# Squares of the decay in a bidirectional gated linear recurrence: from GpSimd with two places to ScalarE with four

## What is computed

```python
def rglru_gates(u, wa, ba, wx, bx, lam):
    r = sigmoid(blockdiag(u, wa) + ba)
    i_g = sigmoid(blockdiag(u, wx) + bx)
    log_a = -LRU_C * r * softplus(-lam)
    a = exp(log_a)
    b = sqrt(-expm1(2.0 * log_a)) * (i_g * u)
    return a, b
# h_t = a_t * h_(t-1) + b_t, over the context first, then over the latent tokens,
# once forwards and once backwards; the two results are added and gated
```

## Time and profile before

| | |
|---|---|
| median of 3 runs | 2322.23 us (2318.98 to 2324.4) |
| profiled execution, its own time | 2321.31 us |
| its span, first to last instruction | 2319.5 us |
| mean granted TensorE clock | 0.92 |
| busy share of the span: PE, DVE, ACT, POOL | 83%, 49%, 34%, 14% |
| the scan stage in the span | about 1388 to 1575 us |

### The profile page before, as it was taken

One profiled execution on the slowest core, in us unless ns is written; L12 is line 12 of the kernel. 1 busy time (PEld: TensorE's weight loads), 2 busy tenths in 40 slices (PEclk: granted clock), 3 DMA queues, 4 the chain that ended last, 5 costly groups with the idle time before them and its releaser, 6 DMA issues. The chain is left out here.

```text
span 2319.5 us, 33553 instructions
## 1 busy us (share of the span) xinstructions
PE 1913.9 (83%) x9971; PEld 1296.5 (56%) x9972; DVE 1148.0 (49%) x2243; ACT 792.0 (34%) x1283; POOL 317.4 (14%) x333
## 2 busy tenths in 40 slices
PE   2899997889999999999975887637778787788883
PEld 0778844467777777777742881103445555555551
DVE  2325622577777777777748565893131121111124
ACT  1214511155555556555521456870101111111110
POOL 0220010021211111121110102221001111111110
PEclk9999997989999999999987997768879999999997
DMA  6850054069999899999956416304439999999994
GB/s 240 282 202 2 1 224 180 32 230 333 340 332 339 324 339 348 346 334 343 336 179 249 136 47 202 110 19 131 183 145 415 407 402 404 404 404 392 409 381 173
DMA packets 139045, 597.07 MB, mean 257 GB/s; under 512 B 32632, under 2 KB 51128, under 8 KB 79728
## 3 DMA queue, kind: packets, MB, share of 16 engines
q1 hardware_dynamic: 103264, 509.97, 58.5%
q0 software_dynamic: 35584, 84.31, 9.8%
q10 hardware_dynamic: 144, 2.10, 0.2%
HBM read 596.17 MB, written 56.20 MB: 281 GB/s over the span
## 5 line engine op out<-in xcount | busy, mean ns | idle before, releaser
L1459 DVE TENSOR_TENSOR m_w_lo<-m_wgu,m_w_hi 128x1024 fp32r<-128x1024 f32 x264 | 314.0, 1221 | 157.3 <-ACT m_w_hi L1383 146.3
L1383 ACT ACTIVATE m_w_hi<-m_wgu 128x1024 fp32r<-128x1024 f32 x264 | 269.7, 1053 | 192.9 <-DMA m_wgu<-in_moe_w_up 135.2
L1630 PE MATMUL ps<-m_wgu,m_xT 128*64 128x256 f32 x2112 | 263.0, 405 | 77.4 <-DMA m_wgu<-in_moe_w_up 57.0
L1630 PEld LDWEIGHTS ps<-m_wgu,m_xT 128*64 128x64 f32 x2112 | 187.3, 146 | 164.0 <-issue 117.2
L1325 PE MATMUL ps<-m_wd,m_hidT 128*128 128x512 f32 x528 | 237.6, 593 | 0.3 <-ACT m_hidT L1407 0.3
L1340 PE MATMUL ps<-m_w_hi,m_x_hi 128*128 128x512 f32 x528 | 212.7, 403 | 7.1 <-DVE m_x_lo L1451 7.0
L1340 PE MATMUL ps<-m_w_lo,m_x_hi 128*128 128x512 f32 x528 | 208.1, 394 | 0.0
L1340 PE MATMUL ps<-m_w_hi,m_x_lo 128*128 128x512 f32 x528 | 207.2, 392 | 0.0
L1725 DVE SCALAR_TENSOR_TENSOR m_hid<-m_act_g,m_meta,ps 128x256 f32<-128x256 f32 x33 | 15.8, 480 | 337.7 <-ACT m_act_g L1679 337.7
L1325 PEld LDWEIGHTS ps<-m_wd,m_hidT 128*128 128x128 f32 x528 | 95.3, 190 | 95.1 <-issue 95.1
L1266 POOL DMA_INDIRECT y_rows<-h,m_sidx x66 | 67.5, 1023 | 552.8 <-DVE h L1467 552.8
(11 more groups left out here) (317 smaller groups left out, 3420.5 us busy)
## 6 DMA issues: line engine op xcount, KB each, us to landing
m_wgu<-in_moe_w_gate SPq DMA_DIRECT2D x132, 1024.0 KB
m_wgu<-in_moe_w_up SPq DMA_DIRECT2D x132, 1024.0 KB
m_wd<-in_moe_w_down SPq DMA_DIRECT2D x132, 1024.0 KB, 9.7
c_rows<-y_rows SPq DMA_DIRECT2D x12, 2048.0 KB, 16.1
mods<-in_ada_w POOLq DMA_DIRECT2D x11, 1024.0 KB, 7.3
mods<-in_ada_w SPq DMA_DIRECT2D x11, 1024.0 KB, 4.8
mods<-in_lru_w_in SPq DMA_DIRECT2D x7, 1280.0 KB, 6.9
ada_w<-in_ada_w SPq DMA_DIRECT2D x8, 1024.0 KB, 17.8
```

Source lines behind the costliest of these rows:

```text
L1383: act.activation(w_hi[:, :, k, :], wgu[:, q, :, k, :], ACT.Copy).then_inc(hi_s, 1)
L1459: dve.tensor_tensor(w_lo[:, :, k, :], wgu[:, q, :, k, :], w_hi[:, :, k, :].bitcast(F32), ALU.subtract).then_inc(lo_s, 1)
L1630: last = pe.matmul(g.ps[half[s], GU, a * FE:(a + 1) * FE], xT[:, k, half[s]], wgu[:, s, a, k, :], start=(k == 0), stop=(k == KD - 1))
```

## The change

ScalarE makes the square of each block's decay right behind its exponential and tangent, with a wait for the complement of block j-4. GpSimd's loop goes away. The squares get a tensor of their own with four places instead of two places in a row of `g.h`.

```diff
-        sq = g.h[0:RW, 2, :].rearrange("p (b c) -> p b c", c=TOK)
+        sq = sb("sq", [RW, 4, TOK])
...
                         act.activation(r[:, q, :], r[:, q, :], ACT.Tanh, bias=pos4[:, c:c + 1], scale=pos4[:, c:c + 1]).then_inc(exps, 1)
+                        if j >= 4:
+                            act.wait_ge(omts, j - 3)
+                        act.activation(sq[:, j % 4, :], a[:, q, :], ACT.Square).then_inc(sqs, 1)
...
-                for j in range(len(blocks)):
-                    n = j % SLOTS
-                    pool.wait_ge(exps, 2 * j + 1)
-                    if j >= 2:
-                        pool.wait_ge(omts, j - 1)
-                    pool.tensor_tensor(sq[:, j % 2, :], a[:, n, :], a[:, n, :], ALU.mult).then_inc(sqs, 1)
...
-                        dve.scalar_tensor_tensor(r[:, j % SLOTS, :], sq[:, j % 2, :], 1.0, r[:, j % SLOTS, :], ALU.add, ALU.mult).then_inc(omts, 1)
+                        dve.scalar_tensor_tensor(r[:, j % SLOTS, :], sq[:, j % 4, :], 1.0, r[:, j % SLOTS, :], ALU.add, ALU.mult).then_inc(omts, 1)
```

## The result

The changed kernel is slower by a ratio of 1.0025 (95% interval 1.0016 to 1.0034), which is +5.8 us on 2320.06 (+3.7 to +7.9). The medians of 20 runs each are 2325.39 and 2320.06 us. The forecast was +5.9 us and 2328.1 us; the three runs shown before the forecast had a median 2.2 us above that of all twenty, and the medians themselves differ by 5.3 us, 0.5 less than the ratio says.

What follows compares the result with a forecast made beforehand. ScalarE was taken to set the pace until VectorE takes over in groups 6 to 8. Squares +12.6, clock +1.6, first `finish` -1.45, groups 6, 7, 8 -2.57, -3.38, -0.9: +5.9 us, 2328.1 us, range 2323 to 2334.

Steps and rivals of the forecast that it cites:

- Price of a square: On ScalarE: 0.525 us a square, 2.10 for four, ends 0.45 and 0.81; 24 squares in the lead, +12.6 us.
- The new wait: On ScalarE before a square, for the complement of block j-4: claimed never to hold.
- Hidden squares: Group 3's squares (2.10 us) fall into block 18's gate-read wait; group 7's are hidden by VectorE's scans.
- Groups 6, 7, 8: Last groups of the scan stage: net shifts of -0.47, -3.38 and -0.9 us as VectorE's work gets shorter.
- First finish: Group 3: scans to `finish` need 8.44 us instead of 9.89, -1.45; block 18's gate-read wait shrinks to 1.2.
- Clock in group 0: TensorE's pause before block 7 grows to 3.35 us, putting that block at the low clock level: +1.6 us.
- rival 1: The clock in group 0 stays high: +4.3 us, 2326.5, a result inside 0.2%; chance 0.22.
- Rivals 2, 3 and 4: Squares dear as tangents, 2332.8 to 2334.9, chance 0.12; VectorE leads from group 4, 2316.4, 0.06; table loads, about 2405, 0.02.
- rival 5: Part of the shift is lost later, where TensorE's clock changes at another instant: 2322 to 2326 us; chance 0.08.

Runs made afterwards that it cites:

- E5: The changed kernel with two places for the squares on ScalarE instead of four; 1.0069 of the kernel before, +16.0 us.
- E1: The kernel before, GpSimd's squares kept, with ScalarE making a second set that nobody reads; ratio 1.004 to the kernel before, +9.3 us.
- E10: The kernel before, unchanged, traced a second time; its scan stage took 147.53 us, group 3 20.32 us.
- E2: The kernel before with the squares left out, the complement reading the decay itself; 0.9959 of the kernel before, -9.5 us.

## Why the prediction was right, step by step

- **Price of a square:** 0.525 forecast, 0.52 measured, 24 of them in the lead: groups 1, 2, 4 and 5 grew by 2.08 each. The new wait never holds (0.0 us); with two places it does (E5).
- **Hidden squares:** those of groups 3, 7 and 8, and in group 6 ScalarE's wait of 2.57 us, which hides its four. E1 confirms it: there they cost nothing in group 3 and in groups 6 to 8.
- **Groups 6, 7, 8:** -0.51, -3.36, -0.80 against -0.47, -3.38, -0.9.
- **First finish:** scans to `finish` took 8.37 us (1472.83 to 1481.20), 8.44 forecast, and block 18's read waited 1.16, 1.2 forecast. What became of it in group 3 depends on the clock. Against the first trace of before, the 1.45 us were gained and 1.4 more from the clock. Against the second, whose reads of blocks 18 and 19 waited 3.92 and 0.46 us, the same sum leaves 0.37 and 0.46; they waited 1.16 and 0.80 in the changed kernel, so 1.1 us went to the clock and 0.33 in all was gained.
- **Clock in group 0: wrong.** The step said that a pause of 3.35 us would put block 7 at the low level, +1.6 us; it cost 0.15. The Trainium skill (TensorE: Matmul & The Clock Gate, section HAM oscillation), by which waits between bursts of matmuls put the clock back for each next burst, agrees with the trace where the next burst started at the low level, after 6.95 and 6.42 us in groups 1 and 2; after 3.33 us the burst started at the high level, and there the measurement decides. What came about was rival 1, and with the other terms as forecast its +4.3 us, "inside 0.2%", would have come. The total was +5.8; against E10 group 3 gave back 0.33 us instead of 1.45. With E10 as the start, the terms are 2.23 + 4 x 2.08 - 0.33 - 0.51 - 3.36 - 0.79 = 5.6 us. So who leads, what a square costs and what VectorE gets back were right, and the clock in groups 0 and 3 was not. That the sum still met the measured change to 0.1 us was luck: two errors, of 1.5 us in group 0 and, against E10, 1.1 us in group 3, cancelled.
- **Rivals 2, 3 and 4** are excluded by the 613 ns and 0.52 us, by E1 and E2, and by the absence of table loads: nine before the roots and eight before the exponentials, as before. The Trainium skill (ScalarE: Activation LUTs, section Table sets) leaves Square out of its list of cheap functions in every set; the trace shows it run from the set of exponential and tangent. Of rival 5, the shift to another clock later on, group 3 showed as much as 2.5 us within one kernel; against E10 it cost the changed kernel 1.1 us of its gain.

## What to carry over

Cut a stage at a fixed instruction of its loop and ask of each piece which engine leads: an operation moved to the leading engine costs its full pitch there, and relief of an engine that follows is worth nothing, even where it is large (2 us of 15 in group 4). Where the lead changes within the stage, split the move: squares by group gave -6.3 us where the whole move gave +5.8. And a place for a result that is enough on an idle engine may be too few on the leading one, where the wait holds up everything behind it.

## What was not expected of the hardware

A pause of TensorE shows in its clock late: behind a busy stretch and a pause of 3.33 us the next matmuls still ran at 2.4 GHz for some 1.6 us and then fell to 1.2 GHz while the engine was at work. (The 1.6 us is an estimate from the product that took 1.31 us, 1.02 at the high level and 1.91 at the low one.) Two executions of the same kernel differed by 2.5 us in one group of the loop, by the instant at which the clock rose again, so two traces alone could not size a change of a few us there. Idle matmuls that kept the clock high in most groups were worth some 8 us to the changed kernel.
